# The image sweep's coefficient cast on VectorE, and the additions of fetched rows behind the coefficients

## What is computed

```python
def block(hb):
    ...
    ids = k1 * PEER_KEYS + k2
    g = jax.nn.softmax(top_s, axis=-1)
    ue = jnp.take(u_tab, ids, axis=0)
    ve = jnp.take(v_tab, ids, axis=0)
    act = jax.nn.gelu(jnp.einsum("nd,nhkd->nhk", hb, ue).astype(jnp.float32))
    return jnp.einsum("nhk,nhkd->nd", (g * act).astype(hb.dtype), ve)
```

## Time and profile before

| | |
|---|---|
| median of 3 runs | 3675.48 us |
| lowest, highest | 3675.16, 3682.06 us |
| the profiled execution | 3677.12 us, its span 3675.3 us |
| busy, whole span | PE 87%, DVE 75%, ACT 35%, POOL 24% |
| image sweep, blocks 12 to 125 | about 1810 to 2516 us of the span |

### The profile page before, as it was taken

One profiled execution on the slowest core, in us unless ns is written; L12 is line 12 of the kernel. 1 busy time (PEld: TensorE's weight loads), 2 busy tenths in 40 slices (PEclk: granted clock), 3 DMA queues, 4 the chain that ended last, 5 costly groups with the idle time before them and its releaser, 6 DMA issues.

```text
span 3675.3 us, 54611 instructions
## 1 busy us (share of the span) xinstructions
PE 3188.5 (87%) x19370; PEld 2725.8 (74%) x19370; DVE 2757.2 (75%) x4857; ACT 1283.3 (35%) x2038; POOL 873.6 (24%) x615
## 2 busy tenths in 40 slices
PE   6997899878984077888989999989989999999998
PEld 3686789657873044777878888878679888888887
DVE  0159976646977698699789999987657987777776
ACT  1111530102511022217544444443343574444443
POOL 0000412323333600000057766654201000000000
PEclk7998999989997579989999999999999999999999
DMA  7643854778986767621599999997545235555554
GB/s 272 214 138 98 269 177 148 288 247 296 312 288 205 262 216 227 205 93 52 183 336 382 385 369 377 380 346 225 168 141 181 81 118 192 189 193 189 189 193 148
DMA packets 246968, 824.25 MB, mean 224 GB/s; under 512 B 40704, under 2 KB 50960, under 8 KB 245536
## 3 DMA queue, kind: packets, MB, share of 16 engines
q1 hardware_dynamic: 136864, 493.41, 39.1%
q0 software_dynamic: 85632, 319.43, 25.1%
q10 hardware_dynamic: 24320, 9.37, 1.0%
HBM read 797.80 MB, written 23.27 MB: 223 GB/s over the span
## 4 chain that ended last, share of the span: by engine, by line
PE 48%; DVE 30%; DMA 14%; issue 6%; POOL 1%; ACT 1%; SPq 0%; DVEq 0%; POOLq 0%; ACTq 0%
PE psum L1354 11%; DMA arena<-in_v,arena 6%; PE psum L765 6%; PE psum L1340 6%; DVE arena L2390 6%; PE psum L1026 4%; PE psum L1459 3%; DMA ring<-in_w 3%; PE psum L1342 3%; DMA stage<-in_u_rows,H 2%; DVE u_split L2961 2%; DVE up_rows L2570 2%; DVE arena L2589 2%; DVE arena L2883 2%; PE psum L1315 2%
## 5 line engine op out<-in xcount | busy, mean ns | idle before, releaser
L1354 PE MATMUL psum<-v_split,coef_split 128*128 128x512 f32 x2856 | 702.1, 395 | 53.0 <-DVE coef_split L3004 52.9
L1354 PEld LDWEIGHTS psum<-v_split,coef_split 128*128 128x128 f32 x2856 | 523.2, 189 | 164.9 <-DVE coef_split L3004 60.5
L595 POOL DMA_INDIRECT arena<-in_v,arena x256 | 449.2, 1755 | 276.0 <-DVE arena L2390 204.9
L2390 DVE SCALAR_TENSOR_TENSOR arena<-arena 128x1024 f32<-128x1024 f32 x254 | 325.1, 1280 | 50.3 <-DMA arena<-in_v,arena 48.4
L1337 PEld LDWEIGHTS psum<-input_split,u_split 128*128 128x128 f32 x2832 | 348.0, 188 | 10.4
L1337 PE MATMUL psum<-input_split,u_split 128*128 128x256 f32 x2832 | 349.6, 279 | 0.0
L1340 PE MATMUL psum<-input_split,u_split 128*128 128x512 f32 x912 | 321.5, 390 | 0.0
L1751 ACT ACTIVATE arena<-psum 128x1024 f32<-128x1024 f32 (+5 forms) x192 | 156.1, 819 | 457.8 <-PE psum L1277 172.7
L2961 DVE TENSOR_TENSOR u_split<-ring,u_split 128x1024 fp32r<-128x1024 f32 x250 | 305.2, 1221 | 6.5 <-ACT u_split L1751 6.4
L765 PE MATMUL psum<-arena,ring 128*128 128x256 f32 x1296 | 293.4, 387 | 11.2 <-ACT arena L1827 4.3
L1751 ACT ACTIVATE u_split<-ring 128x1024 fp32r<-128x1024 f32 x250 | 263.1, 1053 | 110.1 <-DMA ring<-in_u 77.8
(11 more groups left out here) (499 smaller groups left out, 5564.5 us busy)
## 6 DMA issues: line engine op xcount, KB each, us to landing
ring<-in_w SPq DMA_DIRECT2D x420, 512.0 KB, 4.6
ring<-in_u SPq DMA_DIRECT2D x256, 512.0 KB, 3.9
ring<-in_v SPq DMA_DIRECT2D x256, 512.0 KB, 3.6
scratch_inj<-arena ACTq DMA_DIRECT2D x16, 512.0 KB, 3.2
arena<-scratch_inj POOLq DMA_DIRECT2D x7, 1024.0 KB, 8.3
arena<-in_keys POOLq DMA_DIRECT2D x3, 2048.0 KB, 11.4
scratch_cm<-work POOLq DMA_DIRECT2D x8, 512.0 KB, 5.8
scratch_cm<-arena POOLq DMA_DIRECT2D x8, 512.0 KB, 3.7
```

Of the source, the lines that this page charges most:

```text
L595: pool.indirect_dma_start(VROWS[b], None, v_rows, bass.IndirectOffsetOnAxis(ROW_IDS2[:, m:m + 1], 0))\
L1354: last = mm(bank(2 + 2 * i + f), CFR[:, b, c, P * i:P * i + P], parts[:, v, 512 * f:512 * f + 512], start=(first and c == 0 and v == 0), s ...
L2390: ins = stt(acc, VROWS[b], WEIGHTS2[:, m:m + 1], acc, ALU.mult, ALU.add)
```

## The change

On ScalarE `coef_high` goes. On VectorE the written-out coefficient of blocks 12 to 125 becomes a call of `coef`, which has the cast, and the picks of a block all stand behind the low part of u of block j + 2.

```diff
@@ ScalarE @@
-                def coef_high(j, b):
-                    act.wait_ge(sem("gated"), j + (2 * KD_ - e - 1))
-                    act.wait_ge(sem("coef_used"), j + (n0 - 1))
-                    copy(CFR[:, b, 0, :], CT[:, b, :]).then_inc(sem("coef_high"), 1)
...
-                        if p == 0:
-                            coef_high(i * 2 + (e + b), b)
@@ VectorE @@
                     for j in range(e + 2, NEXP - 2):
                         b, some = j % 2, picks_until(j)
                         low(1, j, b, w0 + 2 * j + 2)
-                        dve.wait_ge(sem("gelu_done"), j + 1)
-                        tt(CT[:, b, :], AC[:, b, :], G[:, j, :], ALU.mult).then_inc(sem("gated"), 1)
-                        if made["picks"] < some:
-                            pick()
-                        dve.wait_ge(sem("coef_high"), j - e - 1)
-                        tt(CFR[:, b, 1, :], CT[:, b, :], CFR[:, b, 0, :].bitcast(F32), ALU.subtract)\
-                            .then_inc(sem("coef_ready"), 1)
+                        coef(j, b)
                         low(0, j + 2, b, w0 + 2 * j + 3)
                         while made["picks"] < some:
                             pick()
```

## The result

| | before | changed |
|---|---|---|
| median of the timed runs | 3676.26 us (4 runs, 3675.16 to 3682.06) | 3723.02 us (4 runs, 3721.21 to 3734.25) |
| span of the profiled execution | 3675.3 us | 3721.3 us |
| difference of expert 15 starts at | 1827.55 | 1821.96 |
| difference of expert 126 starts at | 2516.96 | 2563.80 |
| between these two | 689.4 us | 741.8 us |

The changed kernel is slower: ratio 1.013, 95% interval [1.0108, 1.0153], some 47 us. "Difference" is the instruction that writes the coefficient's low part (L3004 of before, for expert 126 L2975; L2969 of the changed kernel). Between those of experts 15 and 126 the sweep grew by 52.4 us, and behind it the two kernels need 1158.3 and 1157.5 us to the end of the span. The 5.6 us by which the profile after reaches expert 15 earlier belong to no change: the same kernel, profiled again on another chip, reached it at 1827.72.

What follows compares the result with a forecast made beforehand. VectorE's issue work plus its waits for rows was taken to set the pace. Added work of 73 us, less credits of 13, 6, 1 and 1, gave +52 us on 3675.5: 3727 us, range 3706 to 3756.

Steps and rivals of the forecast that it cites:

- What bounds the kernel: Image sweep, experts 15 to 126: VectorE sets the pace, 638.9 us of issue work plus 50.7 us of waits.
- VectorE's added work, +73 us: Sweep's 111 experts: 5.99 us with two additions, 7.38 with three; 712.1 us against 638.9.
- Experts 12 to 14, costed at nothing: Experts without additions, where TensorE sets the pace: no cost; 1.4 us if uncovered.
- Self-waits have a price: VectorE: 0.12 us behind the product, 0.19 between neighbouring additions; the rival of free self-waits, 3694 us, had 5 in 100.
- Middle, credit 13 us: Mid-sweep: of 18.6 us waited for rows, all but 6 given back; bounds all 18.6, or no credit.
- The interpolated landing of 7.4 us: Mid-sweep rows: landing falls from 7.9 to 7.4 us as traffic drops from 378 to 350 GB/s.
- the 6 us of new waits: Mid-sweep: rows 0.2 us short of their window, once in each of 28 triples of additions.
- Opening, credit 6 us: 1826.5 to 1910, few buffers open: 5 experts' 0.66 us covered, half of 8 x 0.66; bounds 0 and 14.6.
- Reloads and end: Wait behind the parked-data reloads: credit 1 us (0 to 2); sweep's last coefficients: credit 1 us (0 to 2.75).
- The prediction's lower end: Whole sum with every wait credit at its bound: 73 - 18.6 - 14.6 - 3 = +37 us, 3712 us.
- The cast and GpSimd's port: GpSimd's refills: the cast might delay each by up to 0.29 us, 8 us over 28 triples; nothing added.
- Signs that were off: Trace after: DMA share about 0.93, TensorE's waits for the coefficient growing to some 0.8 us an expert.

Runs made afterwards that it cites:

- the second profile: The changed kernel unaltered, run and profiled again on another chip: 3727.44 us, ratio 1.0144 to the kernel before.
- e9: Kernel before with five row buffers, every addition but the first summing only columns 0 to 63 of 1024: 3629.88 us, ratio 0.9883.
- e10: Changed kernel with five row buffers, every addition but the first summing only columns 0 to 63 of 1024: 3635.01 us, ratio 0.99.
- e6: Changed kernel with a fifth row buffer: 3719.54 us, ratio 1.0124 to the kernel before.
- e7: Kernel before with a fifth row buffer: 3653.45 us, ratio 0.9939.
- e3: Changed kernel with each expert's first addition moved between the coefficient and the low part of u: 3712.02 us, ratio 1.0104 to the kernel before.
- e2: Kernel before with only the cast moved to VectorE, the first addition staying between product and cast: 3699.11 us, ratio 1.0071.
- e1: Kernel before with only the order changed, all additions behind the low part of u, cast still on ScalarE: 3734.54 us, ratio 1.0166.

## Why the prediction was right

The forecast was 3727 us, +52; the time rose by 47 (48 by the ratio, 40 to 56), the sweep by 52.4 in the first profile and 51.0 in the second. The forecast is the sweep's sum, and there it is met; the 5 us by which the times rose less are within their interval, and the first profile has as much ahead of the sweep.

- **What bounds the kernel.** VectorE's issue time plus its waits for rows: borne out by e9 and e10, where with VectorE unburdened the same change is nearly free.
- **VectorE's added work, +73 us.** The steps came out within 0.02 us (5.98 and 7.36 us an expert for 5.99 and 7.38). Experts 12 to 14, costed at nothing, cost nothing: the differences of experts 12 and 15 are 16.57 us apart in both kernels. With rows out of the way (e6 against e7) the middle shows 0.63 us an expert, for 0.66. e3 shows the part of the neighbours, e2 that of the cast (with 0.07 us of its 0.40 from the longer difference).
- **Self-waits have a price.** 0.12 us behind the product and 0.19 between additions are in the rows after as in the earlier trace rows. e3 took one of the 0.19 away, and the addition that starts a new accumulator doesn't pay it; the 0.12 us no run takes apart. The Trainium skill's "VectorE: DVE Perf Modes", section "The DRAIN you can't avoid", has measured copies, for which a semaphore after each cost nothing extra. Carried over to instructions that depend on each other, as here, this case disagrees: 1.39 against 1.20 us.
- **Middle, credit 13 us.** The interpolated landing of 7.4 us was 6.9, though the traffic came to 351 GB/s, as reckoned; the 6 us of new waits were 3.2 (1910 to 2460), in the second profile 1.8. The middle grew by 43.6 us, in the second profile by 40.2, for a forecast of some 90 x 0.66 - 13 = 46. So the credit was 16 to 19 us, nearer to its upper bound of 18.6 than to 13. That the fall in load outweighed the shorter window fits the landing of 6.9 us; no run parts the two.
- **Opening, credit 6 us.** Experts 15 to 28 took 93.8 us instead of 89.8: +4.0 for a forecast of 13 x 0.66 - 6 = +2.6. The second profile has +4.4. The credit was 4 to 5 us, and that the guess of one half came near it was luck.
- **Reloads and end.** The wait is 12.93 us instead of 13.31 (forecast 12), and behind the sweep's last coefficients 0.8 us were regained (forecast 1). The prediction's lower end takes off 3 us for these two, but its own bounds for them, 2 and 2.75, come to 4.75; the end would be +35 instead of +37.
- **The cast and GpSimd's port.** A cast that lengthens GpSimd's issues was left out of the sum, and nothing of it is seen. 94 issues of the changed kernel begin 0.06 us into the product and last through the cast; they took 1.17 us, as did the 13 of before that begin at the same place, where an addition follows. The other way round something small is seen: 2 of the 111 casts took 0.48 and 0.34 us instead of 0.29, both with a transfer instruction of GpSimd of 0.94 us still running when they began, 0.24 us in all. The rule that the prediction had weighed is that of the Trainium skill's "SBUF — State Buffer", section "Who interferes with whom", by which a cast can contend with GpSimd for a port. A refill held up by the cast, the price that the prediction had named, doesn't show in this trace.
- **Signs that were off.** The DMA share was to fall to 0.93 and fell to 0.96, and TensorE's waits for the coefficient were to grow to 0.8 us an expert and grew to 0.55. Neither enters the sum.
- **What the forecast missed.** I had not seen that the two halves of the change work against each other (e1 and e2). The sum was right because I took `coef` as one piece from a row where it stood as one; a sum of separate prices, the order's and the cast's, would have been 89 us.

## What to carry to other kernels

Where an engine has no hole, price an edit by the distance from start to start of its instructions in a row that already has the new sequence, self-waits included, and then ask separately which waits the slower pace gives back. An instruction that stands between a request to another engine and the use of its answer is cover: moving it away changes where the request is cheapest. And before taking a full-looking resource for the bound, give the waiting engine one more buffer: here a few lines away from the change lay 30 us.

## What I had not expected of the hardware

- The DMA share stood at 1.00 at 378 GB/s (before), 1.01 at 392 (e7) and 1.02 at 408 (e9): a share of 1.00 is not yet the ceiling.
- Where a row's issue on GpSimd and a low part or difference on VectorE begin within some 0.03 us of each other, one of the two is longer. In e2, 105 differences took 0.49 us instead of 0.42 and the issues 0.94. In before, 94 low parts of u kept their 1.22 us and the issues took 2.01, while 9 low parts took 1.27 and the issues 0.94. What decides between the two is open.
- GpSimd's issue of a row transfer took 1.49 us in the mean beside the changed kernel's VectorE and 1.80 before. That isn't the bunching, since it took 1.32 in e2, which has no more neighbours than before. It goes with the place where an issue begins: in the changed kernel 98 issues began 0.17 us into an addition and took 1.93 us, the 94 at the product 1.17, and 18 beside an idle VectorE 0.94. The first two kinds ended 0.81 us after the VectorE instruction at whose side they had begun.
